# Three projections of the second block in three passes on split operands in place of float32

## The chip, the cores and the metric

The kernel runs on one core of a Trainium2 chip. The metric is the device time of one execution in microseconds, lower is better. Engines are named as in the profile: PE is TensorE (PEld its weight loads), DVE is VectorE, ACT is ScalarE, POOL is GpSimd, SP is SyncE, which here only issues DMAs.

## The reference, cut to what matters

Two transformer blocks follow each other on 512 tokens of width 1024. The change is in the second one's mixer, behind its two attention branches:

```python
def hybrid_mixer(h, positions, w_in, ...):
    ...
    q_lat, kv_lat, k_rope, q_b, k_b, v_b, gate_a, gate_b = jnp.split(h @ w_in, cuts, axis=-1)
    ...
    o_a = mla_attend(q_a, k_a, v_a)                      # 512 wide
    o_b = chunk_band_attend(q_b, k_b, v_b, rel_table)    # 512 wide
    merged = jax.nn.sigmoid(gate_a) * (o_a @ w_oa) + jax.nn.sigmoid(gate_b) * (o_b @ w_ob)
    return merged @ w_out
```

and in the block, `x = x + gt1 * mix`, then an RMS norm, and a mixture of experts.

## The kernel before

All activations are held transposed, features on the 128 partitions and the 512 tokens along the free axis, so a projection takes a 128x128 piece of weights as the stationary operand and a 128x512 piece of activations as the moving one. Each engine has a program of its own, written out by hand in order; they meet by semaphores alone. SyncE streams weights into `ring`, four slots of 2048 columns: a slot holds 256 output columns for 8 (or 4) k steps of 128 rows. `slot()` waits for a slot's load (`full`), `half` (L572) runs one 128-column half of it, `kts` matmuls into one PSUM bank, and counts `half_done`. The load of slot m + 4 waits until both halves of slot m are done. ACT and DVE empty the banks and count `freed["A"]` and `freed["D"]`, for which a later half on the same bank waits; `drain_psum` makes PE wait, ahead of a stage, for all evictions of the stages before.

The order around the change: two attentions of 16 units each (`attend(16, ...)`, the latent one, whose output is `OA`, and `attend(32, ...)`, the banded one, whose output is `OB`). Between units PE also computes the latent gates (`lat_gate_matmuls`, L934), and ACT copies them to `LAT_GATE`. Then:

- `mla_out`, 4 slots: `OA` times `w_oa_2`, 4 k steps, 8 halves. DVE multiplies each with its sigmoid gate (L2131). PE waits for `outed`, 48, before it.
- `band_out`, 8 slots in 4 groups (`gated_projection`): two halves of the band gate, `hT` times `w_in_2` in 8 k steps, then two halves of `OB` times `w_ob_2` in 4 k steps. ACT takes the sigmoid of the gates (L1365), DVE multiplies and adds into `merged2` (L1900, L1901).
- `w_out2`, 4 slots: `merged2` times `w_out_2`, 8 k steps. DVE adds each half to the residual (`residual`, L2000). The norm of the next part follows.

All of it is float32, and each float32 matmul leaves two records in the trace. The first block's attention projections (L880, L904) and its feed-forward part (L1031, L1060) already work in another way: a weight w and an operand x are each held as a rounded part in the type fp32r ("high") and what is left of them ("low"), and three matmuls, low w x high x, high w x low x, high w x high x, take the place of one in float32. There ACT makes the high part of a weight slot (L1383) and DVE the low part in the ring's own slot (L1922); in the feed-forward part GpSimd makes it.

```python
            drain_psum(pe, "w_out2")
            for t in range(4):
                m = slot()
                for hf in range(2):
                    hh = 2 * t + hf
                    if hh >= 4:
                        pe.wait_ge(freed["D"], BEFORE["w_out2"]["D"] + hh - 3)
                    half(m, hf, hh % 4, lambda k: merged2[:, k, :])
```

Of the kernel before, what the change touches and what calls it, by code (L numbers as in the profile page):

```python
# [12 lines left out]
F32 = mybir.dt.float32  # L13
# [3 lines left out]
ALU = mybir.AluOpType  # L17
# [132 lines left out]
def build(nc, a, stop=99):  # L150

    with ExitStack() as ctx:
# [6 lines left out]
        def sem(name):  # L159
            return ctx.enter_context(nc.semaphore(name))  # L160
# [86 lines left out]
        BROW = area(33280, 640)  # L247
        merged2, gate2 = area(6656, KT, T), area(12800, 2, T)
        LAT_GATE = [area(4096 + i * T, T) for i in range(4)] + [area(10752 + i * T, T) for i in range(4)]
        H2T = area(4096, 4, D)  # L250
        XE = area(8192, 2, 8, 2 * SLOTS)
        PICKED = area(10240, 2, 4, 2 * SLOTS)
# [46 lines left out]
        y_made, mean_made, var_made, g_made = sem("y_made"), sem("mean_made"), sem("var_made"), sem("g_made")  # L299
        y_added, centred, y_sq, y_root, y_final = [sem(n) for n in (  # L300
            "y_added", "centred", "y_squared", "y_rooted", "y_final")]
        gate_ready, lat_gate = sem("gate_ready"), sem("latent_gate_ready")
        scored, masked, peaked, probbed, turned, turnedS, weighed, outed, diag_made = [sem(n) for n in (
            "scored", "masked", "peaked", "probbed", "turned", "turned_copied", "weighed", "outed", "diagonal_made")]
# [253 lines left out]
        def _(pe):  # L558
            n = [0]

            def slot():
                m = n[0]
                n[0] += 1
                pe.wait_ge(full[m % R], full_value(m))
                return m
# [267 lines left out]
            pe.wait_ge(y_final, 8)  # L833


            def gated_projection(phase, rhs, kts):
                drain_psum(pe, phase)
                for g in range(4):
                    m = slot()
                    for hf in range(2):  # L840
                        i = 2 * g + hf
                        if i >= 2:
                            pe.wait_ge(freed["A"], BEFORE[phase]["A"] + i - 1)
                        half(m, hf, i % 2, h_)
                    m = slot()
                    for hf in range(2):
                        i = 2 * g + hf
                        if i >= 2:
                            pe.wait_ge(freed["D"], BEFORE[phase]["D"] + i - 1)
                        half(m, hf, 2 + i % 2, rhs, kts=kts)  # L850

            for g in range(4):
                m = slot()
# [265 lines left out]
            attend(32, parts_band, PROB2, PROBT2, gates_beside=2)  # L1119
            pe.wait_ge(outed, 48)  # L1120
            for g in range(4):
                m = slot()
                for hf in range(2):
                    i = 2 * g + hf
                    if i >= 4:
                        pe.wait_ge(freed["D"], BEFORE["mla_out"]["D"] + i - 3)
                    half(m, hf, i % 4, lambda k: OA[:, k, :], kts=4)
            gated_projection("band_out", lambda k: OB[:, k, :], 4)
            drain_psum(pe, "w_out2")
            for t in range(4):  # L1130
                m = slot()
                for hf in range(2):
                    hh = 2 * t + hf
                    if hh >= 4:
                        pe.wait_ge(freed["D"], BEFORE["w_out2"]["D"] + hh - 3)
                    half(m, hf, hh % 4, lambda k: merged2[:, k, :])
            norm_sum(4)
            pe.wait_ge(normed, 5)
            if stop < 6:
# [87 lines left out]
        def _(act):  # L1227
# [124 lines left out]
                if t < 8:  # L1352
                    y_square(t)

            def gates(phase):

                for g in range(4):
                    for hf in range(2):
                        i = 2 * g + hf
                        act.wait_ge(half_done, 2 * FIRST[phase] + 4 * g + hf + 1)  # L1360
                        if i >= 2:
                            act.wait_ge(freed["D"], BEFORE[phase]["D"] + i - 1)
                        elif i == 0:
                            act.wait_ge(freed["D"], BEFORE[phase]["D"])
                        act.activation(gate2[:, i % 2, :], ps[:, i % 2, :], ACT.Sigmoid, bias=ZERO).then_inc(freed["A"], 1)  # L1365

            act.wait_ge(y_final, 8)
            act.activation(C2S, col("c_2", 0, 8), ACT.Silu).then_inc(silu_c, 1)
            act.wait_ge(freed["A"], BEFORE["rw_out"]["A"] + 8)
# [49 lines left out]
            def attend(u0, parts_of, prob, probT, gates_beside=False):  # L1419
                def exp(i, e):  # L1420
                    u = u0 + i
                    pt = parts_of(pairs[i], i)
                    act.wait_ge(peaked, u + 1)
                    p_ = prob[i % 2][e][:, 0:pt["tiles"] * P]
                    act.activation(p_, p_, ACT.Exp, scale=pt["scale"], bias=NM[:, i % 2, e:e + 1],  # L1425
                                   accum_out=DEN[:, i % 2, e:e + 1]).then_inc(probbed, 1)

                def copies(i, e):
                    u = u0 + i
                    n_ = parts_of(pairs[i], i)["tiles"]  # L1430
                    if u >= 2:
                        act.wait_ge(weighed, u - 1)
                    for t_ in range(0, n_, 4):
                        g = turn_n[0]
                        turn_n[0] += 1
                        k = min(4, n_ - t_)
                        act.wait_ge(turned, g + 1)
                        act.activation(probT[i % 2][e][:, t_ * P:(t_ + k) * P], ps[:, 5 + g % 2, 0:k * P],
                                       ACT.Copy).then_inc(turnedS, 1)

                exp(0, 0)
                exp(0, 1)
                for i in range(len(pairs)):
                    for e in range(2):
                        if i + 1 < len(pairs):
                            exp(i + 1, e)
                        copies(i, e)
                    if gates_beside and i % 4 == 3:
                        lat_gate_copy()

            attend(0, parts1, PROB1, PROBT1)
            if stop < 4:
# [110 lines left out]
            attend(32, parts_band, PROB2, PROBT2, gates_beside=True)  # L1563
            act.wait_ge(freed["A"], BEFORE["mla_out"]["A"] + 8)
            for i in range(8):
                act.activation(LAT_GATE[i], LAT_GATE[i], ACT.Sigmoid, bias=ZERO).then_inc(lat_gate, 1)
            gates("band_out")
# [120 lines left out]
        def _(dve):  # L1688
# [202 lines left out]
                    y_centre(t - 1)  # L1891
                ada_rest(2 * t + 1)

            def gated(phase, gate, merged):

                for i in range(8):
                    g, hf = divmod(i, 2)
                    dve.wait_ge(half_done, 2 * FIRST[phase] + 4 * g + 2 + hf + 1)
                    dve.wait_ge(freed["A"], BEFORE[phase]["A"] + i + 1)
                    lk.done(tt(gate[:, i % 2, :], ps[:, 2 + i % 2, :], gate[:, i % 2, :], ALU.mult))  # L1900
                    tt(merged[:, i, :], merged[:, i, :], gate[:, i % 2, :], ALU.add).then_inc(freed["D"], 1)  # L1901
# [41 lines left out]
            def attend(u0, parts_of, prob, OT):  # L1943
                def peaks(i):
                    u = u0 + i
                    pt = parts_of(pairs[i], i)
# [26 lines left out]
                for i in range(len(pairs)):  # L1973
                    if i + 1 < len(pairs):
                        peaks(i + 1)
                    if i >= 1:
                        outs(i - 1)
                    denominators(i)
                outs(len(pairs) - 1)

            dve.wait_ge(got_masks, 16)
# [145 lines left out]
            attend(32, parts_band, PROB2, [OB[:, k, :] for k in range(4)])  # L2127
            for i in range(8):
                dve.wait_ge(half_done, 2 * FIRST["mla_out"] + 8 + i + 1)
                dve.wait_ge(lat_gate, i + 1)  # L2130
                tt(merged2[:, i, :], ps[:, i % 4, :], LAT_GATE[i], ALU.mult).then_inc(freed["D"], 1)  # L2131
            gated("band_out", gate2, merged2)
# [194 lines left out]
```

## Time and profile before

| what | value |
|---|---|
| median of 3 runs | 2627.1 us (2624.62 to 2631.7) |
| the profiled execution | 2626.47 us, its span 2624.7 us |
| mean granted TensorE clock | 0.951 of full speed |
| PE busy | 2365.8 us (90%) |
| PE weight loads busy | 1626.4 us (62%) |
| DVE busy | 1036.6 us (39%) |
| ACT busy | 618.3 us (24%) |
| POOL busy | 219.5 us (8%) |
| the three stages of the change | 2030.63 to 2198.58 us |

A busy PE says that matmuls are in flight, not that they run at the engine's best pace, so the rows below give counts and lengths for the stages. The span runs from the first to the last instruction; the device time is a little longer.

### The profile page before, as it was taken

How to read it: one execution, taken by the hardware profiler on the slowest of the kernel's cores; microseconds unless marked ns; L12 is line 12 of the kernel's file. 1: busy time of each engine (PE TensorE's matmuls, PEld its weight loads, DVE VectorE, ACT ScalarE, POOL GpSimd, SP SyncE). 2: the span in 40 equal slices, each digit the busy share in tenths (PEclk: the TensorE clock that was granted, in tenths of full speed). 3: DMA queues.
4: the chain of work that ended last, by engine and by line, in shares of the span. 5: the costliest groups of instructions: out<-in, count | busy, mean ns of one | idle time of the engine just before them, and what ended most of it. 6: DMA issues, size and time to landing. Idle time of an engine off the chain costs nothing.

```text
span 2624.7 us, 41843 instructions
## 1 busy us (share of the span) xinstructions
PE 2365.8 (90%) x18202; PEld 1626.4 (62%) x18202; DVE 1036.6 (39%) x1878; ACT 618.3 (24%) x922; POOL 219.5 (8%) x97
## 2 busy tenths in 40 slices
PE   8889999999789999889599989789899997899992
PEld 7376859584338898554388868436355443777771
DVE  0264554535565562441477740130544111311113
ACT  1213232312502222540333321210345001111111
POOL 0010101010000000000244334100000000000001
PEclk9899999999899999899799999899999998899996
DMA  6211010104464652003133322441200220699992
GB/s 203 79 35 34 19 49 4 49 13 137 144 206 153 192 183 91 1 31 114 32 97 96 96 72 89 84 100 44 92 17 17 88 76 0 212 361 374 369 339 104
DMA packets 273606, 295.19 MB, mean 112 GB/s; under 512 B 7593, under 2 KB 257361, under 8 KB 273457
## 3 DMA queue, kind: packets, MB, share of 16 engines
q1 hardware_dynamic: 268080, 274.85, 32.4%
q0 software_dynamic: 3072, 9.74, 1.8%
q10 hardware_dynamic: 2304, 8.39, 0.8%
q8 instruction: 122, 2.00, 0.3%
q14 instruction: 28, 0.22, 0.0%
HBM read 279.84 MB, written 13.11 MB: 112 GB/s over the span
## 4 chain that ended last, share of the span: by engine, by line
PE 80%; DVE 11%; ACT 4%; issue 2%; DMA 2%; POOL 0%; SPq 0%; POOLq 0%; DVEq 0%; ACTq 0%
PE ps L572 20%; PE ps L1031 9%; PE ps L661 9%; PE ps L880 7%; PE ps L1060 5%; PE ps L1175 4%; PE ps L1193 4%; PE ps L904 3%; PE ps L589 2%; PE ps L934 2%; PE ps L1212 2%; PE ps L598 2%; PE ps L950 2%; PE ps L962 1%; DVE arena L1951 1%
## 5 line engine op out<-in xcount | busy, mean ns | idle before, releaser
L572 PE MATMUL ps<-hT,ring 128*128 128x512 f32 (+1 forms) x816 | 359.1, 599 | 17.5 <-DVE hT L1740 16.0
L572 PEld LDWEIGHTS ps<-hT,ring 128*128 128x128 f32 (+1 forms) x816 | 154.8, 191 | 218.6 <-issue 200.7
L572 PE MATMUL ps<-arena,ring 128*128 128x512 f32 (+1 forms) x592 | 262.4, 602 | 14.7 <-DVE arena L2105 6.4
L661 PE MATMUL ps<-arena 64*64 64x64 f32 x7168 | 226.1, 221 | 16.2 <-POOL arena L1630 8.8
L661 PEld LDWEIGHTS ps<-arena 64*64 64x64 f32 x7168 | 221.0, 137 | 21.0 <-POOL arena L1630 9.6
L572 PEld LDWEIGHTS ps<-arena,ring 128*128 128x128 f32 (+1 forms) x592 | 111.8, 190 | 160.4 <-issue 146.0
L1636 POOL TENSOR_TENSOR w_low<-ring,w_high 128x2048 fp32r<-128x2048 f32 x22 | 103.8, 4721 | 869.9 <-ACT w_high L1466 869.9
L1031 PE MATMUL ps<-h_high,w_low 128*128 128x512 f32 x352 | 140.2, 398 | 24.2 <-DVE h_low L2010 24.2
L1031 PE MATMUL ps<-h_high,w_high 128*128 128x512 f32 x352 | 140.7, 400 | 0.0
L1031 PE MATMUL ps<-h_low,w_high 128*128 128x512 f32 x352 | 139.3, 396 | 0.0
L1175 PE MATMUL ps<-arena 128*128 128x128 f32 x1088 | 130.5, 279 | 2.9 <-DVE arena L2207 2.9
L1175 PEld LDWEIGHTS ps<-arena 128*128 128x128 f32 x1088 | 125.9, 194 | 9.1 <-issue 6.1
L1193 PE MATMUL ps<-ring,arena 128*64 128x256 f32 x1024 | 118.7, 380 | 2.3 <-DMA ring<-in_w_up 1.5
L1951 DVE CUSTOM_DVE_ANT_0 arena<-ps,arena 128x256 f32<-128x256 f32 (+3 forms) x160 | 67.1, 468 | 128.2 <-PE ps L950 128.0
L880 PE MATMUL ps<-h_high,w_low 128*128 128x512 f32 x256 | 103.1, 403 | 13.1 <-DVE w_low L1922 12.7
L1268 ACT ACTIVATE arena<-ps 128x512 f32<-128x512 f32 x104 | 62.1, 597 | 210.9 <-PE ps L661 200.7
L1193 PEld LDWEIGHTS ps<-ring,arena 128*64 128x64 f32 x1024 | 87.5, 137 | 37.0 <-issue 9.6
L1776 DVE TENSOR_TENSOR arena<-ps,arena 128x512 f32<-128x512 f32 x88 | 60.9, 692 | 119.2 <-PE ps L661 119.1
L2032 DVE TENSOR_TENSOR rstd<-arena 128x512 f32<-128x512 f32 x22 | 98.4, 4473 | 17.5 <-ACT arena L1497 17.5
L880 PE MATMUL ps<-h_low,w_high 128*128 128x512 f32 x256 | 102.3, 400 | 0.0
L880 PE MATMUL ps<-h_high,w_high 128*128 128x512 f32 x256 | 101.9, 398 | 0.0
L1425 ACT ACTIVATE arena<-arena,small 128x384 f32<-128x384 f32 (+6 forms) x96 | 68.0, 708 | 114.9 <-DVE small L1959 114.9
(328 smaller groups left out, 3535.9 us busy)
## 6 DMA issues: line engine op xcount, KB each, us to landing
ring<-in_w_in SPq DMA_DIRECT2D x54, 1024.0 KB, 5.2
arena<-in_w_ada SPq DMA_DIRECT2D x80, 512.0 KB, 4.0
ring<-in_w_gate SPq DMA_DIRECT2D x32, 1024.0 KB, 10.4
ring<-in_w_up SPq DMA_DIRECT2D x32, 1024.0 KB, 11.8
arena<-in_w_down SPq DMA_DIRECT2D x32, 1024.0 KB, 9.2
ring<-in_w_up SPq DMA_DIRECT2D x44, 512.0 KB, 4.5
ring<-in_w_ada SPq DMA_DIRECT2D x8, 1024.0 KB, 8.7
ring<-in_w_down SPq DMA_DIRECT2D x8, 1024.0 KB, 5.0
```

The costliest lines, as they stand in the source:

```text
L572: mm = pe.matmul(dst, w[:, k, hf * P:hf * P + width], rhs(k), start=(start and k == 0), stop=(stop and k == kts - 1))
L661: mm = pe.matmul(ps[r, bank, cc], l[r, cc], x[r, 0:64] if x is eye64 else x[r, cc], start=(i == 0), stop=(i == len(terms) - 1))
L880: mm = pe.matmul(ps[:, bank, :], w_[:, k, hf * P:hf * P + P], x_[:, k, :], start=(k == 0 and i_ == 0), stop=(k == KT - 1 and i_ == 2))
L904: mm = pe.matmul(ps[:, hh % 4, tt * 256:tt * 256 + 256], x_[:, k, tok:tok + P], w_[:, k, :], start=(k == 0 and i_ == 0), stop=(k == KT - 1 ...
L1031: mm = pe.matmul(ps[:, (2 * (m - first) + g) % 4, :], w_[:, k, :], x_[:, k, :], start=(k == 0 and i_ == 0), stop=(k == KT - 1 and i_ == 2))
L1060: mm = pe.matmul(ps[:, hh % 4, :], w_[:, k, hf * P:hf * P + P], x_, start=(kt == 0 and i_ == 0), stop=(kt == FT - 1 and i_ == 2))
L1175: mm = pe.matmul(ps[:, hf, k * P:k * P + P], H2T[:, tt, (4 * hf + k) * P:(4 * hf + k + 1) * P], PICKED[:, par, tt, :], start=(tt == 0), st ...
L1193: mm = pe.matmul(ps[e * SLOTS:(e + 1) * SLOTS, 2 + part, 0:256], XE[:, j, k, e * SLOTS:(e + 1) * SLOTS], w[:, k, :], start=(k == 0), stop= ...
L1425: act.activation(p_, p_, ACT.Exp, scale=pt["scale"], bias=NM[:, i % 2, e:e + 1], accum_out=DEN[:, i % 2, e:e + 1]).then_inc(probbed, 1)
L1636: pool.tensor_tensor(W_LOW[:, slot_, :], ring[:, slot_, :], W_HIGH[:, j % 2, :].bitcast(F32), ALU.subtract).then_inc(w_low, 1)
L1951: dve.tensor_tensor_reduce(out=prob[i % 2][e][:, at:at + mask.shape[1]], in0=out, in1=mask, scale=1.0, scalar=NEG, op0=ALU.add, op1=ALU.ma ...
L2032: tt(val, sil[:, jj % 2, :], cvt[jj % 2][1], ALU.mult).then_inc(dve_link, 1)
```

## The change

The three stages' float32 matmuls become three fp32r matmuls each. Every weight slot and every 128x512 piece of `OA`, `hT` (called H3), `OB` and `merged2` (M2) is split first: ACT copies it to fp32r, DVE subtracts that from it and writes the low part in place. `out_weight(i)` names the 16 slots (0 to 3 `mla_out`, 4 to 11 `band_out` with even ones the gates' and odd ones `OB`'s, 12 to 15 `w_out2`); slots 0 to 3 and `OB`'s have 1024 columns, the others 2048. The high parts take turns in two small buffers (0 to 3) and two large ones (4 to 15), so the cast of weight i waits until PE is done with weight i - 2. `OA`'s pieces and the weights 0 and 1 are split within the band attention; the rest is written into the programs of ACT and DVE among their evictions. PE waits for `out_w_low` at each slot and for `piece_low` at each k step.

```diff
+        OUT_W_HIGH = ([rounded(f"w_small_{i}", offset_of["arena"] + (13824 + i * 1024) * 4, SLOT // 2)[:, :] for i in range(2)]
+                      + [rounded(f"w_large_{i}", offset_of["arena"] + (16896 + i * SLOT) * 4, SLOT)[:, :] for i in range(2)])
...
+        def out_weight(i):
+
+            m = FIRST["mla_out"] + 4 + i
+            size = SLOT // 2 if i < 4 or (i < 12 and i % 2 == 1) else SLOT
+            high = OUT_W_HIGH[i % 2 + (2 if i >= 4 else 0)]
+            return m, high[:, 0:size], ring[:, m % R, 0:size], W_LOW[:, m % R, 0:size]
...
+            def out_slot(i):
+
+                slot()
+                pe.wait_ge(out_w_low, i + 1)
...
+            def out_half(w, hf, bank, pieces, first_piece):
+
+                wl, wh = w
+                n_ = len(pieces)
+                for k, (_, high, low) in enumerate(pieces):
+                    pe.wait_ge(piece_low, first_piece + k + 1)
+                    for i_, (w_, x_) in enumerate(((wl, high), (wh, low), (wh, high))):
+                        mm = pe.matmul(ps[:, bank, :], w_[:, k, hf * P:hf * P + P], x_,
+                                       start=(k == 0 and i_ == 0), stop=(k == n_ - 1 and i_ == 2))
+                mm.then_inc(half_done, 1)
...
             drain_psum(pe, "w_out2")
             for t in range(4):
-                m = slot()
+                w = out_slot(12 + t)
                 for hf in range(2):
                     hh = 2 * t + hf
                     if hh >= 4:
                         pe.wait_ge(freed["D"], BEFORE["w_out2"]["D"] + hh - 3)
-                    half(m, hf, hh % 4, lambda k: merged2[:, k, :])
+                    out_half(w, hf, hh % 4, M2_PIECES, PIECE_AT["M2"])
```

ACT's new program (in the band attention it also makes `OA`'s pieces after units 2, 4, 6, 8 and weights 0 and 1 after units 12 and 14):

```diff
+            def out_weight_high(i):
...
+                act.wait_ge(full[m % R], full_value(m))
+                if i >= 2:
+                    act.wait_ge(half_done, 2 * (m - 2) + 2)
+                act.activation(high, full_, ACT.Copy).then_inc(out_w_high, 1)
...
+            act.wait_ge(outed, 48)
+            for g in range(4):
+                for i in range(2 * g, 2 * g + 2):
+                    act.activation(LAT_GATE[i], LAT_GATE[i], ACT.Sigmoid, bias=ZERO).then_inc(lat_gate, 1)
+                for k in range(2 * g, 2 * g + 2):
+                    high_piece(H3_PIECES[k])
+                if g == 1:
+                    for k in range(4):
+                        high_piece(OB_PIECES[k])
+                out_weight_high(g + 2)
+            for g in range(4):
+                for hf in range(2):
+                    i = 2 * g + hf
+                    act.wait_ge(half_done, 2 * FIRST["band_out"] + 4 * g + hf + 1)
...
+                    act.activation(gate2[:, i % 2, :], ps[:, i % 2, :], ACT.Sigmoid, bias=ZERO).then_inc(freed["A"], 1)
+                out_weight_high(6 + 2 * g)
+                for k in range(2 * g - 2, 2 * g) if g else ():
+                    high_piece(M2_PIECES[k])
+                out_weight_high(7 + 2 * g)
+            for k in range(6, 8):
+                act.wait_ge(freed["D"], BEFORE["band_out"]["D"] + k + 1)
+                high_piece(M2_PIECES[k])
+            out_weight_high(14)
+            out_weight_high(15)
```

DVE's new program (in the band attention, low parts after units 3, 5, 7, 9 and 13, 15):

```diff
+            def out_weight_low(i):
...
+                dve.wait_ge(out_w_high, i + 1)
+                tt(low, full_, high.bitcast(F32), ALU.subtract).then_inc(out_w_low, 1)
...
+            for g in range(4):
+                for k in range(2 * g, 2 * g + 2):
+                    low_piece(H3_PIECES[k])
+                for i in range(2 * g, 2 * g + 2):
+                    dve.wait_ge(half_done, 2 * FIRST["mla_out"] + 8 + i + 1)
+                    dve.wait_ge(lat_gate, i + 1)
+                    tt(merged2[:, i, :], ps[:, i % 4, :], LAT_GATE[i], ALU.mult).then_inc(freed["D"], 1)
+                if g == 1:
+                    for k in range(4):
+                        low_piece(OB_PIECES[k])
+                out_weight_low(g + 2)
+            for g in range(4):
+                out_weight_low(6 + 2 * g)
+                for k in range(2 * g - 2, 2 * g) if g else ():
+                    low_piece(M2_PIECES[k])
+                for i in range(2 * g, 2 * g + 2):
+                    dve.wait_ge(half_done, 2 * FIRST["band_out"] + 4 * g + 2 + i % 2 + 1)
+                    dve.wait_ge(freed["A"], BEFORE["band_out"]["A"] + i + 1)
+                    lk.done(tt(gate2[:, i % 2, :], ps[:, 2 + i % 2, :], gate2[:, i % 2, :], ALU.mult))
+                    tt(merged2[:, i, :], merged2[:, i, :], gate2[:, i % 2, :], ALU.add).then_inc(freed["D"], 1)
+                out_weight_low(7 + 2 * g)
+            low_piece(M2_PIECES[6])
+            low_piece(M2_PIECES[7])
+            out_weight_low(14)
+            out_weight_low(15)
             residual("w_out2", mod2[:, 16:24])
```

## Rows read from the trace of the kernel before

**Rows 1.** The page: busy time, share of the span and instructions of each engine.

```profile
PE 2365.8 (90%) x18202; PEld 1626.4 (62%) x18202; DVE 1036.6 (39%) x1878; ACT 618.3 (24%) x922; POOL 219.5 (8%) x97
```

**Rows 2.** Stretches: length, busy PE, PEld, DVE, ACT, POOL, clock, DMA share, GB/s.

```profile
2030.60:2059.00 28.40, 27.73 (x64) 12.08 (x64) 5.43 (x8) 5.67 (x9) 0.00 (x0) 1.00 0.36 110
2059.00:2142.00 83.00, 82.64 (x192) 36.40 (x192) 9.90 (x16) 5.50 (x8) 0.00 (x0) 1.00 0.26 83
2142.00:2199.00 57.00, 55.17 (x128) 24.24 (x128) 6.91 (x10) 0.00 (x0) 2.86 (x4) 1.00 0.09 24
```

**Rows 3.** Chain of waits in the three stages: start, length (us), what.

```profile
2030.63 27.73 PE ps L572 x64
2059.20 82.64 PE ps L572 x192
2143.39 55.19 PE ps L572 x128
```

**Rows 4.** Chain of waits in earlier projections: split ones, and `w_uk_2`.

```profile
1023.43 22.52 PE ps L880 x96
...
1289.02 249.01 PE ps L1031 x1056
...
1880.06 7.01 PE ps L1113 x16
```

**Rows 5.** Groups by line and shape, of three stretches: busy us, mean ns.

```profile
L880 PEld LDWEIGHTS ps<-h_low,w_high 128*128 128x128 f32 x256 | 48.7, 190 | 11.2
...
L1909 DVE TENSOR_TENSOR h_low<-hT,h_high 128x512 fp32r<-128x512 f32 x8 | 5.1, 682 | 0.0
...
L1373 ACT ACTIVATE h_high<-hT 128x512 fp32r<-128x512 f32 x8 | 4.2, 612 | 0.0
...
L2032 DVE TENSOR_TENSOR rstd<-arena 128x512 f32<-128x512 f32 x22 | 98.4, 4473 | 17.5 <-ACT arena L1497 17.5
...
L2000 DVE SCALAR_TENSOR_TENSOR arena<-ps,small,arena 128x512 f32<-128x512 f32 x8 | 6.0, 750 | 50.1 <-PE ps L572 50.1
...
L1900 DVE TENSOR_TENSOR arena<-ps,arena 128x512 f32<-128x512 f32 x8 | 5.5, 690 | 72.9 <-PE ps L572 72.9
L1365 ACT ACTIVATE arena<-ps,small 128x512 f32<-128x512 f32 x8 | 5.5, 687 | 93.9 <-PE ps L572 93.9
```

**Rows 6.** Order of time at two hand-overs: start, length, what [idle before].

```profile
857.02 0.40 PE L880 MATMUL ps<-h_high,w_high 128*128 128x512 f32 x1
...
857.52 1.92 ACT L1383 ACTIVATE w_high<-ring 128x2048 fp32r<-128x2048 f32 x1 [5.06 <-PE ps L880]
...
859.47 2.29 DVE L1922 TENSOR_TENSOR w_low<-ring,w_high 128x2048 fp32r<-128x2048 f32 x1 [1.32 <-ACT w_high L1383]
...
2142.60 0.69 DVE L1901 TENSOR_TENSOR arena<-arena 128x512 f32<-128x512 f32 x1
```

**Rows 7.** Order of time in the attention's last units.

```profile
2021.77 0.40 ACT L1425 ACTIVATE arena<-arena,small 128x128 f32<-128x128 f32 x1 [2.11 <-DVE small L1959]
...
2024.12 0.29 DVE L1951 CUSTOM_DVE_ANT_0 arena<-ps,arena 128x128 f32<-128x128 f32 x1 [1.34 <-PE ps L950]
...
2029.96 0.29 DVE L1969 COPY arena<-ps 128x128 f32<-128x128 f32 x1 [1.53 <-PE ps L980]
```

**Rows 8.** DMA issues, 2025 to 2200 us: count, KB each, us to landing.

```profile
ring<-in_w_in SPq DMA_DIRECT2D x4, 1024.0 KB, 5.2
```

**Rows 9.** After pauses: TensorE's next matmul, chain of waits, stretches (PEclk).

```profile
613.07 1.13 PE L799 MATMUL ps<-arena,const 128*128 128x512 f32 x2 [3.24 <-DVE arena L1869]
...
1256.03 8.85 PE ps L589 x16
...
2203.05 10.08 PE ps L589 x16
...
610.00:616.00 6.00, 2.93 (x6) 0.97 (x6) 4.68 (x10) 0.00 (x0) 0.00 (x0) 1.00 0.56 175
...
2203.00:2209.00 6.00, 5.95 (x7) 2.52 (x8) 0.00 (x0) 1.28 (x1) 0.00 (x0) 0.50 0.00 0
```

More of the change, by code:

```diff
@@ L301, in build @@
             "y_added", "centred", "y_squared", "y_rooted", "y_final")]
+        out_w_high, out_w_low, piece_high, piece_low = [sem(n) for n in (
+            "out_weights_high", "out_weights_low", "piece_high_made", "piece_low_made")]
         gate_ready, lat_gate = sem("gate_ready"), sem("latent_gate_ready")
@@ L833, in _ @@
             pe.wait_ge(y_final, 8)
-            def gated_projection(phase, rhs, kts):
-                drain_psum(pe, phase)
-                for g in range(4):
-                    m = slot()
[L840 to L850, printed above, removed]
+            def out_slot(i):
+                slot()
+                pe.wait_ge(out_w_low, i + 1)
+                _, high, _, low = out_weight(i)
+                return [v.rearrange("p (k c) -> p k c", c=256) for v in (low, high)]
+            def out_half(w, hf, bank, pieces, first_piece):
[7 more added lines that the diff above has]
+                mm.then_inc(half_done, 1)
             for g in range(4):
@@ L1121, in _ @@
             for g in range(4):
-                m = slot()
+                w = out_slot(g)
                 for hf in range(2):
@@ L1126, in _ @@
                         pe.wait_ge(freed["D"], BEFORE["mla_out"]["D"] + i - 3)
-                    half(m, hf, i % 4, lambda k: OA[:, k, :], kts=4)
-            gated_projection("band_out", lambda k: OB[:, k, :], 4)
+                    out_half(w, hf, i % 4, OA_PIECES, PIECE_AT["OA"])
+            drain_psum(pe, "band_out")
+            for g in range(4):
+                w = out_slot(4 + 2 * g)
+                for hf in range(2):
+                    i = 2 * g + hf
+                    if i >= 2:
+                        pe.wait_ge(freed["A"], BEFORE["band_out"]["A"] + i - 1)
+                    out_half(w, hf, i % 2, H3_PIECES, PIECE_AT["H3"])
+                w = out_slot(5 + 2 * g)
+                for hf in range(2):
+                    i = 2 * g + hf
+                    if i >= 2:
+                        pe.wait_ge(freed["D"], BEFORE["band_out"]["D"] + i - 1)
+                    out_half(w, hf, 2 + i % 2, OB_PIECES, PIECE_AT["OB"])
             drain_psum(pe, "w_out2")
             for t in range(4):
-                m = slot()
+                w = out_slot(12 + t)
                 for hf in range(2):
@@ L1353, in _ @@
                     y_square(t)
[L1355 to L1365, printed above, removed]
             act.wait_ge(y_final, 8)
@@ L1449, in attend @@
                         lat_gate_copy()
+                    if split_beside and i in (2, 4, 6, 8):
+                        act.wait_ge(outed, u0)
+                        high_piece(OA_PIECES[i // 2 - 1])
+                    if split_beside and i in (12, 14):
+                        out_weight_high(i // 2 - 6)
             attend(0, parts1, PROB1, PROBT1)
@@ L1892, in _ @@
                 ada_rest(2 * t + 1)
[L1894 to L1901, printed above, removed]
             for i in range(8):
@@ L1941, in _, with low_piece, attend @@
             lk.done(tt(mod2, ps[:, 6, 32:80], col("b_ada_2", 0, 48), ALU.add))
-            def attend(u0, parts_of, prob, OT):
+            def out_weight_low(i):
+                if i >= 16:
+                    return
+                _, high, full_, low = out_weight(i)
+                dve.wait_ge(out_w_high, i + 1)
+                tt(low, full_, high.bitcast(F32), ALU.subtract).then_inc(out_w_low, 1)
+            pieces_n = [0]
+            def low_piece(piece):
+                pieces_n[0] += 1
+                dve.wait_ge(piece_high, pieces_n[0])
+                tt(piece[2], piece[0], piece[1].bitcast(F32), ALU.subtract).then_inc(piece_low, 1)
+            def attend(u0, parts_of, prob, OT, split_beside=False):
                 def peaks(i):
@@ L1978, in attend @@
                     denominators(i)
+                    if split_beside and i in (3, 5, 7, 9):
+                        low_piece(OA_PIECES[i // 2 - 1])
+                    if split_beside and i in (13, 15):
+                        out_weight_low(i // 2 - 6)
                 outs(len(pairs) - 1)
@@ L2126, in _ @@
             attend(16, parts_mla, PROB2, [OA[:, k, :] for k in range(4)])
[L2127 to L2132, printed above, removed]
+            attend(32, parts_band, PROB2, [OB[:, k, :] for k in range(4)], split_beside=True)
+            for g in range(4):
[9 more added lines that the diff above has]
+                out_weight_low(g + 2)
+            for g in range(4):
+                out_weight_low(6 + 2 * g)
[11 more added lines that the diff above has]
+            out_weight_low(15)
             residual("w_out2", mod2[:, 16:24])
```

29 lines of the change are left out of this document (24 added, 5 removed).

## The prediction

> **What bounds the kernel now.** I read the page first: TensorE works for 2365.8 us, 90% of the span [rows 1]. The table of stretches then shows that in the three stages that the change touches (2030.6 to 2199 us) TensorE is busy without a break at a granted clock of 1.00, while VectorE works 22 and ScalarE 11 of 168 us, and the DMA engines are a third used or less [rows 2]. The chain of waits has the stages as three pieces of TensorE work: 27.73 us for the 32 matmuls of `mla_out` (a float32 matmul leaves two records, so x64), 82.64 us for the 96 of `band_out`, 55.19 us for the 64 of `w_out2`, with pauses of 0.83 and 1.55 us between [rows 3]. So the stretch from 2030.63 to 2198.58, 167.95 us, is as long as its matmuls, 165.56 us for 192 of them, 0.862 us each. What counts is (a) how long the new matmuls take and (b) whether the splitting, all of it new work for ScalarE and VectorE, keeps ahead of them.
>
> **The matmuls.** Each of the 192 becomes three of the kind that the first block already runs: 96 of them in 22.52 us, which is 0.2346 us each, and 1056 in 249.01, 0.2358 [rows 4]. 576 x 0.2346 = 135.1 us, against 165.6: 30.4 us less. I take 0.2346 because its row has no cold start in it. The order and the tile shapes are those of the first block's helper.
>
> The new passes are not as cheap as the old ones: a fourth of 0.862 is 0.2155, and at that price 576 would take 124.1, another 11.0 less. That is a rival below. The Trainium skill ("FP8 and Floating Point Precision", TensorE Precision Notes) says that true float32 is four passes through the array, and the reduced form reads float32 and truncates; counted by passes alone, three for four would save a quarter, 41.4 us. Rows of this kernel say 30.4, and the rows decide.
>
> Each half now also has a wait ahead of every group of three matmuls, 192 in all, on semaphores that have mostly fired. The row of 96 in [rows 4] runs over two weight slots and four halves, with their waits on slot, splitting and bank, at full pace; and eight matmuls of `w_uk_2` with a wait ahead of nearly each take 7.01 us, 0.876 each against 0.862 [rows 4, 3], so at most 0.014 us a wait, 2.7 us for 192. I take 0.
>
> **The splitting, beside the matmuls.** Prices: ScalarE casts 128x512 in 0.61 and 128x2048 in 1.92 us; VectorE subtracts 128x512 in 0.68 and 128x2048 in 2.29 [rows 5, 6]; in proportion between those, 128x1024 takes 1.05 and 1.22. A gate's sigmoid is 0.69, each of VectorE's two operations on a half 0.69 [rows 5]. Handing over costs little: a half's last matmul (857.02, 0.40 long) ends 0.10 before ScalarE's cast starts, VectorE starts 1.95 after the cast started; from VectorE's last addition (2142.60 + 0.69) to the next matmul is 0.10 [rows 6, 3].
>
> Added in all: 24 operand pieces and 16 weights (eight of 1024, eight of 2048 columns): ScalarE 24 x 0.61 + 8 x 1.05 + 8 x 1.92 = 38 us, VectorE 24 x 0.68 + 8 x 1.22 + 8 x 2.29 = 44. Beside 11 and 22 us of old work this is far below 135 us, so the sum fits; what decides is order. I walk it, with 0 at 2030.63 (the last output of the attention). A slot of four k steps is 24 matmuls, 5.63 us; of eight, 11.26.
>
> Within the attention lie OA's four pieces and weights 0 and 1. Their longest pieces, 1.05 on ScalarE and 1.22 on VectorE, stand after units in which ScalarE sits idle 2.11 us and VectorE 1.34 and 1.53 [rows 7]. Cost taken: 0; were all of it exposed, 4 x 1.29 + 2 x 2.27 = 9.7. TensorE starts at 0, as before.
>
> `mla_out`: slots end at 5.63, 11.26, 16.89, 22.52. Weight 2 may be cast once slot 0 is used: 5.73, ready 8.0, wanted at 11.26. Weight 3: ScalarE waits for slot 1, 11.36, VectorE first makes two H3 pieces, two evictions and OB's four, and is ready at 16.0, wanted at 16.89. Weight 4 (2048 columns): slot 2 ends 16.89, cast from 17.0, low part 18.95 to 21.25. VectorE then has H3's pieces 6 and 7 (to 22.6) and the last two evictions (to 24.0), for which the next stage waits: TensorE starts `band_out` at 24.1, a pause of 1.6 against 0.83 before.
>
> `band_out`: weight 6 of the next group can be cast only when slot 4 is used, and is wanted one OB slot, 5.63 us, later. In between: 0.10 to ScalarE, a sigmoid 0.69 queued ahead of the cast, 1.95 to VectorE's start, 2.29, 0.10 = 5.13. It fits with 0.5 us to spare, in each of three groups. The other weights have 11 us. The ring's loads start a ring's turn ahead: 5.2 us for 1024 KB [rows 8], against at least 16.9 between a slot's end and its next use; nothing is exposed. Four groups of 16.89 end at 91.7.
>
> Then the queue order bites. Slot 10 ends at 86.0; ScalarE: sigmoid to 86.8, cast of weight 12, VectorE's low part 88.75 to 91.05, M2's pieces 4 and 5 to 92.4, multiplication and addition for two halves, 4 x 0.69, to 95.2; only then may `w_out2` start, at 95.3. The pause is 3.6 us, against 1.55. Weight 13 (ready 97.5) and M2's last pieces (98.9) come while the first half still works on its first six pieces (until 99.6).
>
> In `w_out2` VectorE's program has the low parts of weights 14 and 15 *ahead of* the residual evictions. Weight 15 takes the buffer of weight 13, so its cast waits for slot 13, the second, to end: 95.3 + 22.52 = 117.8. Cast from 117.9, low part 119.85 to 122.1, the first residual (0.75 [rows 5]) to 122.9. TensorE wants the first bank again at 117.8, for its fifth half, and gets it at 123.0: a pause of 5.2 us that the kernel before does not have. The last two slots end at 145.5.
>
> Sum: 167.95 - 145.5 = 22.4 us less; that is 30.4 less in matmuls, and pauses of 10.4 (1.6 + 3.6 + 5.2) for 2.4.
>
> **The clock.** TensorE's next work after the stretch pauses 4.5 us (2198.58 to 2203.05) for the squares of the norm; its sixteen float32 records, 6.90 at the pace of [rows 3], then take 10.08, and the stretch 2203 to 2209 shows clock 0.50 of 2.4 GHz, so 1.2 [rows 3, 9]; before the pause TensorE was busy at 1.00 [rows 2]. The same records in the first block, behind the same squares, took 8.85. After a pause of 3.24 us the clock was still 1.00 [rows 9]. So the pause of 5.2 us costs a further 1.95 to 3.2; I take 2.4. The one of 3.6 lies between the rows: 0 to 3.2, I take 1.1.
>
> The Trainium skill ("TensorE: Matmul & The Clock Gate", What's actually happening) says that the gate runs freely, not in step with the kernel. By that rule either pause may cost more in one run than in another; the trace agrees in that two such pauses cost 1.95 and 3.2.
>
> **The forecast.** 22.4 - 2.4 - 1.1 = 18.9 us less. The profiled execution took 2626.47 (span 2624.7), the median of the runs is 2627.1. 2626.5 - 18.9 = 2607.6; set toward the median, 2608.0.
>
> **Rivals.**
> *The passes at the old pace.* 0.2155 instead of 0.2346: 2597. Against it stand both split rows of [rows 4]. 6 in 100.
> *Starved of weights.* A subtraction-like operation of 512 columns takes VectorE 4.47 us where GpSimd works beside it [rows 5]. If a weight's low part took as long here, the chain in `band_out` would be 7.3 for a cover of 5.63: three times 1.7, and 2.2 more in each of the three pauses that have one in them, 11.7 in all: 2620. GpSimd is idle here [rows 2], so the full price is unlikely; a part of it, or some us lost in the attention, gives 2611 to 2618. 14 in 100.
> *The pauses hide.* If an eviction comes earlier than walked, or the clock holds, up to 6 us come back: 2602 to 2604. 8 in 100.
> *Slower: the waits between triples.* If a wait keeps the next weights from loading under the matmul before, the load (0.19 [rows 5]) and a hop (0.10) are bare, 192 x 0.29 = 56 us: 2664. It turns into a loss from 18.9 / 192 = 0.10 us a wait. That row allows 0.014 [rows 4]. 4 in 100.
> *No change:* only if one of these just eats 18.9. 2 in 100.
> The walk as it stands, 2604 to 2612: 66 in 100.
>
> A difference under 0.3% (7.9 us) can't be told from none here. Faster by more: 94 in 100. The range runs from 2601, which leaves out the cheap passes, to 2616, which leaves out the upper end of the starved case and the slower one.
>
> **What would show it.** In the profile after: the 576 matmuls at 0.2333 to 0.236 apart; a pause ahead of each of the two later stages near 1.6 and 3.6 us; one of about 5.2 us four halves into `w_out2`, ended by VectorE's residual, with the low part of weight 15 just before it; clock 0.50 behind it for some us; no pause inside `band_out`; the attention as long as before. The prediction is wrong if `band_out` shows a pause at each group, if the triples stand apart by more than 0.71 us, or if TensorE starts `mla_out` later than now.

## The result, and the profile after

The changed kernel took 2602.32 us in the median of 4 runs (2596.43 to 2604.45), against 2627.53 for the kernel before (4 runs, 2624.62 to 2631.7): a ratio of 0.9899 (0.9877 to 0.9921), or 26.5 us less (20.8 to 32.3); the two medians are 25.2 us apart. The forecast was 2608.0 with a range from 2601 to 2616, set from a sum of 18.9 us less; against the 2627.1 it started from, the range is 26.1 to 11.1 us less. As a time 2602.32 lies in the range; as a saving by the ratio, 26.5 lies just outside it. A second comparison, with five more runs of the changed kernel and 17 of the one before, gave 0.9929 (0.9916 to 0.9942), 18.7 us less, close to the forecast. Both have to be explained. One of the 17 took 2854.59 us, at a mean granted clock of 0.822 where the others had 0.95, and no ratio counts it.

The profiled execution of the changed kernel took 2600.65 us, its span 2598.9. Its chain of waits (start, length, what) through the three stages, which answers to [rows 3]:

```profile
1874.53 7.01 PE ps L1139 x16
...
2025.10 22.65 PE ps L874 x96
...
2049.01 67.42 PE ps L874 x288
2116.42 3.22 issue
2119.64 22.63 PE ps L874 x96
2142.36 1.92 ACT w_large L1454
2144.30 2.29 DVE w_low L2010
2147.51 24.81 PE ps L874 x96
2173.14 3.62 ACT hT L1271
```

The stages run from 2025.10 to 2172.32, 147.22 us, where they took 167.95: 20.7 us less. There are three pauses. The one ahead of `band_out` is 1.26 us (2025.10 + 22.65 to 2049.01), that ahead of `w_out2` 3.22, and the one in the middle of `w_out2` lies between 2142.27 and 2147.51, 5.24 us, with the cast of weight 15 and then its low part in it. The two pieces of 96 matmuls in `w_out2` are the same work, yet one took 22.63 and the other 24.81. And `mla_out` starts 5.5 us earlier than before. The attention is not the reason: from the first matmul of `w_uk_2`'s group (L1139) to the start of `mla_out` it is 150.57 us, in [rows 3, 4] as well (1880.06 to 2030.63).

VectorE's queue around the two later pauses, with ScalarE's cast of weight 12, in order of time (start, length, instruction, idle before it):

```profile
2111.46 1.91 ACT L1454 ACTIVATE w_large<-ring 128x2048 fp32r<-128x2048 f32 x1
...
2113.39 2.29 DVE L2010 TENSOR_TENSOR w_low<-ring,w_large 128x2048 fp32r<-128x2048 f32 x1 [9.51 <-ACT w_large L1454]
2115.60 1.28 DVE L2018 TENSOR_TENSOR merged_low<-arena,merged_high 128x512 fp32r<-128x512 f32 x2
...
2116.81 0.68 DVE L2227 TENSOR_TENSOR arena<-ps,arena 128x512 f32<-128x512 f32 x1
...
2118.85 0.69 DVE L2228 TENSOR_TENSOR arena<-arena 128x512 f32<-128x512 f32 x1
...
2144.30 2.29 DVE L2010 TENSOR_TENSOR w_low<-ring,w_large 128x2048 fp32r<-128x2048 f32 x1 [8.89 <-ACT w_large L1454]
2146.51 2.72 DVE L2081 SCALAR_TENSOR_TENSOR arena<-ps,small,arena 128x512 f32<-128x512 f32 x4
```

This is the chain that was walked: weight 12's low part, two pieces of M2, the four operations of the last two halves, and TensorE starts 0.10 after the last; later, weight 15's low part with all the residuals behind it. The stretches show the clock, in the columns of [rows 2]:

```profile
2119.60:2147.50 27.90, 22.62 (x96) 17.97 (x97) 8.84 (x7) 4.43 (x3) 2.85 (x4) 0.96 0.12 26
2147.50:2153.00 5.50, 5.49 (x14) 4.39 (x15) 1.73 (x3) 0.00 (x0) 0.00 (x0) 0.57 0.00 0
2153.00:2173.00 20.00, 19.31 (x83) 15.20 (x81) 2.90 (x4) 0.00 (x0) 0.00 (x0) 1.00 0.00 0
```

Behind the pause of 5.2 us TensorE works 5.5 us at a mean of 0.57, at 1.2 GHz for most of it, and then at 1.00 again. Behind the one of 3.22 there is nothing of the kind: the 96 matmuls there take 22.63 us, like the 96 of `mla_out`.

### The profile page after: what moved, and what is told of

Same layout as the page of the kernel before. It is cut to its first block, busy times and chain, and to the rows that moved or that the text cites. A ratio compares the mean times of both kernels' runs of the same rounds, so it can differ in the third digit from the quotient of the medians.

```text
span 2598.9 us, 42348 instructions
## 1 busy us (share of the span) xinstructions
PE 2333.0 (90%) x18394; PEld 1660.6 (64%) x18394; DVE 1076.9 (41%) x1918; ACT 653.6 (25%) x962; POOL 219.3 (8%) x97
## 4 chain that ended last, share of the span: by engine, by line
PE 79%; DVE 11%; ACT 4%; issue 2%; DMA 2%; POOL 0%; SPq 0%; POOLq 0%; DVEq 0%; ACTq 0%
PE ps L596 14%; PE ps L1057 10%; PE ps L685 9%; PE ps L906 7%; PE ps L874 5%; PE ps L1086 5%; PE ps L1214 4%; PE ps L1232 4%; PE ps L930 3%; PE ps L613 2%; PE ps L960 2%; PE ps L1251 2%; PE ps L622 2%; PE ps L976 2%; DVE arena L2028 1%
## 5 line engine op out<-in xcount | busy, mean ns | idle before, releaser
L596 PE MATMUL ps<-hT,ring 128*128 128x512 f32 (+1 forms) x688 | 304.5, 602 | 16.7 <-DVE hT L1810 16.0
L596 PEld LDWEIGHTS ps<-hT,ring 128*128 128x128 f32 (+1 forms) x688 | 131.0, 191 | 187.3 <-issue 169.4
L596 PE MATMUL ps<-arena,ring 128*128 128x512 f32 (+1 forms) x336 | 149.8, 603 | 12.4 <-DVE arena L2186 6.4
L596 PEld LDWEIGHTS ps<-arena,ring 128*128 128x128 f32 (+1 forms) x336 | 62.9, 189 | 95.7 <-issue 82.4
L906 PE MATMUL ps<-h_high,w_low 128*128 128x512 f32 x256 | 102.6, 401 | 13.6 <-DVE w_low L1983 13.1
## 6 DMA issues: line engine op xcount, KB each, us to landing
ring<-in_w_gate SPq DMA_DIRECT2D x32, 1024.0 KB, 10.4
```

The source lines that it names most:

```text
L596: mm = pe.matmul(dst, w[:, k, hf * P:hf * P + width], rhs(k), start=(start and k == 0), stop=(stop and k == kts - 1))
L906: mm = pe.matmul(ps[:, bank, :], w_[:, k, hf * P:hf * P + P], x_[:, k, :], start=(k == 0 and i_ == 0), stop=(k == KT - 1 and i_ == 2))
```

## The experiments

Eight runs, two of the known kernels again and six of new ones, in two groups: a0, a1, e1 and e2 beside a kernel before with a median of 2626.87 us, e3, e4, e5 and e7 beside one of 2625.27. The stage length is that of the chain, from the first matmul of `mla_out` to the end of the last piece of `w_out2`.

| kernel | `mla_out` starts | stages | median us | ratio to before |
|---|---|---|---|---|
| before | 2030.63 | 167.95 | 2627.53 | 1 |
| after | 2025.10 | 147.22 | 2602.32 | 0.9899 (0.9877 to 0.9921) |
| a0_before_again | 2027.49 | 167.95 | 2623.28 | 0.9991 (0.9981 to 1.0002) |
| a1_after_again | 2032.17 | 147.22 | 2607.53 | 0.9929 (0.9916 to 0.9942) |
| e1_low15_after_residual3 | 2030.60 | 139.61 | 2597.79 | 0.9891 (0.9875 to 0.9906) |
| e2_w_out2_float32 | 2031.91 | 148.07 | 2605.58 | 0.9921 (0.9908 to 0.9933) |
| e3_filled_pause | 2032.11 | 144.88 | 2603.16 | 0.9909 (0.9891 to 0.9927) |
| e4_evictions_first | 2032.42 | 139.72 | 2594.62 | 0.9883 (0.9866 to 0.9901) |
| e5_one_wait_per_half | 2031.94 | 147.23 | 2605.67 | 0.9922 (0.9904 to 0.9940) |
| e7_low_parts_by_gpsimd | 2029.95 | 153.00 | 2606.44 | 0.9916 (0.9897 to 0.9936) |

**Both kernels again.** No edit.

> The kernel before, once more. The profile of after reached the first matmul of `mla_out` 5.5 us earlier than that of before (2025.10 against 2030.63), though nothing in the program ahead of it differs but the splitting inside the band attention. Theory A (chance): stretches that start on a slow TensorE clock run shorter or longer from one execution to the next, so this profile may reach `mla_out` anywhere from 2024 to 2033 us, and the ratio to before is 1.000. Theory B (the change itself moves the first part): this profile has `mla_out` at 2030.6 again, within 1 us, and every profile with the change at 2025.

> The changed kernel, once more, in five rounds. Theory A: the stretch from the first matmul of `mla_out` to the last of `w_out2` is 147.2 us again within 1 us (167.95 before), so 20.7 us is what the change is worth, and the ratio comes nearer to 1 - 20.7/2627 = 0.992 than to the first 0.9899; `mla_out` starts anywhere from 2019 to 2030 us. Theory B: the ratio stays at 0.990 and `mla_out` starts at 2025 again.

The stages are 167.95 and 147.22 us again, to the hundredth, while their start moved: to 2027.49 in the kernel before, to 2032.17 in the changed one, where before it was the changed one that was early. The eight profiles with the change or a version of it start `mla_out` between 2025.10 and 2032.42, the two without at 2027.49 and 2030.63. So the 5.5 us are chance, and theory B falls. The range expected for the changed kernel, 2019 to 2030, was too low: 2032.17 lies outside it.

Most of what separates the two profiles of the changed kernel at `mla_out`, 7.1 us, comes from one pause far ahead of the change. Near 610 us TensorE waits for VectorE, and then runs a few matmuls, up to those of L815. The first profile, and then the second, with its stretch there in the columns of [rows 2]:

```profile
610.74 1.13 PE L823 MATMUL ps<-arena,const 128*128 128x512 f32 x2 [3.28 <-DVE arena L1939]
615.69 0.98 PE ps L815 x28
```

```profile
613.81 2.07 PE L823 MATMUL ps<-arena,const 128*128 128x512 f32 x2 [3.28 <-DVE arena L1939]
623.30 1.01 PE ps L815 x28
613.80:623.30 9.50, 9.49 (x12) 2.91 (x14) 3.75 (x8) 0.00 (x0) 0.00 (x0) 0.50 0.59 176
```

After the same pause of 3.28 us the clock stayed at 1.00 in one profile and fell to 0.50 in the other, and the same work took 4.95 us in one and 9.49 in the other. This is the pause of 3.24 us that the prediction read in the kernel before [rows 9]. In the ten profiles of this document it is 3.17 to 3.47 us long; the clock held behind it in three (before, a0, after) and fell in the seven others, at a price of 1.7 to 4.5 us.

Between the kernel before and the first profile of the changed one that pause makes no difference. A part of their 5.5 us can be seen in the first attention (stretches of the kernel before, and then of the changed one, from the last projection slots ahead of it to the first matmul behind it):

```profile
1023.40:1167.10 143.70, 120.21 (x1002) 88.39 (x1001) 62.13 (x291) 68.15 (x135) 0.00 (x0) 0.95 0.04 12
```

```profile
1018.70:1159.80 141.10, 117.41 (x1002) 87.09 (x1001) 62.12 (x291) 67.95 (x135) 0.00 (x0) 0.98 0.04 12
```

The same 1002 records of matmuls, VectorE and ScalarE busy for the same time within 0.2 us; the clock was 0.95 in one and 0.98 in the other, and 2.6 us went with it. In the second profile of the changed kernel this stretch is 143.5 us at 0.95. The lead of the first profile goes up and down on the way: 3.1 us at the first projection (72.23 against 75.34), 0.7 at 223.35, 4.7 at 1018.71, 7.3 at 1159.80, 5.5 at `mla_out`. The first projection begins at 72.2 to 72.3 in seven of the eight changed kernels, and at 75.3 to 75.7 in e1 and both profiles of the kernel before. Whether that has to do with the program is open. Near 224 us, at the third of these projection pieces, 0.3 to 2.4 us are left of it: the eight start it at 221.96 to 223.73, the two of the kernel before at 224.06 and 224.34.

**The low part of weight 15 behind the residuals.**

```diff
-            out_weight_low(15)
-            residual("w_out2", mod2[:, 16:24])
+            residual("w_out2", mod2[:, 16:24], between=lambda: out_weight_low(15))
```

with `between` called ahead of the fifth residual.

> VectorE makes the low part of weight 15 after the fourth residual, not ahead of the first. The walk's account: the pause of 5.25 us halfway through `w_out2` goes, and with it the slow clock behind it (x96 in 24.81 against 22.63), so the stages take 147.2 - 5.25 - 2.2 = 139.8 us, and the kernel 7.4 us less than with the change alone. Rival (the pause is due to the bank or to slot 14's weights, not to the order of VectorE's queue): a pause of 3 to 5 us stays, and less than 2 us is won.

The chain of waits of this kernel in `w_out2`:

```profile
2121.94 3.22 issue
2125.16 45.05 PE ps L874 x192
```

192 matmuls in one piece: the pause is gone and the clock's price with it. The stages take 139.61 us, expected 139.8. The rival falls. The medians of e1 and a1, which ran in one group, are 9.7 us apart, where the stages give 7.6; another 2.3 lie behind the stages, which the expectation did not count: from the end of `w_out2` to the end of the span it is 424.0 us in e1 and 426.3 in a1, and the 16 matmuls behind the norm's pause (L613) take 8.84 us against 10.20.

**`w_out2` in float32.**

```diff
-                w = out_slot(12 + t)
+                m = slot()
...
-                    out_half(w, hf, hh % 4, M2_PIECES, PIECE_AT["M2"])
+                    half(m, hf, hh % 4, lambda k: merged2[:, k, :])
```

with the pieces of M2 and the weights 12 to 15 no longer split.

> Only `w_out2` goes back to float32; `mla_out` and `band_out` stay split. By the walk `w_out2`'s part of the change has eaten itself up: 10.1 us won in 192 fp32r matmuls for 64 float32 ones, 5.25 lost in the pause, 2.2 to the clock, 1.7 more pause ahead of the stage. So the stages take 91.3 + 1.6 + 55.2 = 148.1 us, within 1 us of the changed kernel's 147.2, and the times can't be told apart. Rival (each stage brings its share of the 20.7 us, a third of the matmuls a third of the gain): 7 to 10 us slower than the changed kernel.

The stages take 148.07 us, 0.85 more than with `w_out2` split: a third of the new matmuls brings 4% of the gain. The rival falls. The saving in matmuls is 55.19 - 45.29 = 9.9 us (22.63 and, without the slow clock, 22.66 from e3); 5.24 goes back in the pause within the stage, 1.66 in the longer pause ahead of it, and 2.15 to the clock. The ratios, 0.9921 and 0.9929, can't be told apart.

**The pause filled.** Ahead of the wait of `w_out2`'s fifth half:

```diff
+                    if hh == 4:
+                        for _ in range(20):
+                            pe.matmul(ps[:, 5, :], M2_HIGH[:, 0, 0:P], M2_HIGH[:, 0, :], start=True, stop=True)
```

> As the changed kernel, but TensorE runs 20 matmuls of 512 columns into an unused bank while it would pause halfway through `w_out2`. The pause before the fifth half stays as long, since VectorE sets it, but TensorE isn't idle in it. If the 2.2 us that the half stretch behind the pause takes over the others (24.8 against 22.6) are the slow clock, they go: that piece takes 22.6, the stages 145.0 against 147.2, and the granted clock stays at 1.00. Rival (they are slot 14's or 15's weights coming late): 24.8 stays.

TensorE's and the other engines' instructions in order of time there:

```profile
2149.12 4.71 PE L1175 MATMUL ps<-merged_high 128*128 128x512 f32 x20
2149.38 1.92 ACT L1457 ACTIVATE w_large<-ring 128x2048 fp32r<-128x2048 f32 x1 [9.28 <-PE ps L874]
2151.32 2.29 DVE L2013 TENSOR_TENSOR w_low<-ring,w_large 128x2048 fp32r<-128x2048 f32 x1 [8.90 <-ACT w_large L1457]
2153.54 2.72 DVE L2084 SCALAR_TENSOR_TENSOR arena<-ps,small,arena 128x512 f32<-128x512 f32 x4
2154.33 0.50 PE L874 MATMUL ps<-merged_high,w_low 128*128 128x512 f32 x1 [0.51 <-DVE arena L2084]
```

and its chain behind the pause:

```profile
2154.33 22.66 PE ps L874 x96
```

The wait is as long as it was (2149.12 to 2154.33, 5.2 us), but with TensorE at work in it the next 96 matmuls take 22.66 us and not 24.8, and the granted clock is 1.00 in both stretches, as expected. So the 2.2 us were the clock's, and nothing late is behind them. 144.88 us, expected 145.0.

**Evictions first.** The edit of e1, and VectorE's order in the last groups: in `mla_out` the pieces 6 and 7 of H3 behind the last two evictions, in `band_out` weight 12 between the evictions of the seventh and the eighth half, and the rest behind both, with TensorE's waits counted to match:

```diff
+                if g == 3:
+                    for k in range(6, 8):
+                        low_piece(H3_PIECES[k])
...
+                    if i == 7:
+                        out_weight_low(12)
...
+            for k in range(4, 8):
+                low_piece(M2_PIECES[k])
+            out_weight_low(13)
```

> E1, and VectorE also empties banks ahead of what is not yet due: in the last group of `mla_out` both evictions before H3's pieces 6 and 7, in the last group of `band_out` the seventh half's before weight 12's low part and the eighth's right behind it, then M2's pieces 4 to 7, then weight 13. By the walk the pause ahead of `band_out` falls from 1.26 to 0.9, the one ahead of `w_out2` from 3.2 to 2.1: the stages take 138.3 us, 1.5 less than E1. Rival (the low part of weight 12 sets the start alone, so the order of the evictions doesn't matter): the same length as E1 within 0.3 us. The ratio to before should be near 1 - 29.6/2627 = 0.9887 where upstream chance allows.

139.72 us, where 138.3 was expected and e1 had 139.61. By its length alone the rival would have won. The chain says otherwise:

```profile
2032.42 22.65 PE ps L874 x96
...
2055.90 64.64 PE ps L874 x276
...
2124.82 0.70 DVE arena L2237
2125.53 0.09 issue
2125.62 4.51 PE ps L874 x12
```

The pause ahead of `band_out` is 0.83 us (from 2055.07), as expected 0.9. The one ahead of `w_out2` is 2.28, expected 2.1, and 3.22 in e1. But this time the clock fell to 1.2 GHz behind it, as the stretch behind the pause shows:

```profile
2125.60:2128.70 3.10, 3.08 (x7) 2.48 (x8) 3.10 (x5) 0.78 (x2) 2.61 (x4) 0.50 0.87 254
```

The 192 matmuls took 46.52 us, 1.47 more than e1's 45.05. Without that the stages would be 138.25. At this place the pause of 3.22 us, in five profiles (3.21 in e5), never cost clock, and this shorter one did, while the pause of 3.2 to 3.5 us near 610 us cost it in seven of ten. There is one profile of e4, so how often its pause does so is not known, and what the reordering is worth stays open between -0.1 and 1.4 us; the ratio, 0.9883 (0.9866 to 0.9901), is the lowest measured, but it can't be told from e1's.

**Fewer waits.** OA, H3 and OB wait once at each half:

```diff
+                if first_piece < 16:
+                    pe.wait_ge(piece_low, first_piece + n_)
                 for k, (_, high, low) in enumerate(pieces):
-                    pe.wait_ge(piece_low, first_piece + k + 1)
+                    if first_piece >= 16:
+                        pe.wait_ge(piece_low, first_piece + k + 1)
```

> For OA, H3 and OB, TensorE waits for the last piece once at each half instead of for each piece at each k step: 104 of the 192 waits fall away, and all these pieces are ready by then. If a wait that has fired costs nothing between triples, the two pieces of TensorE work keep 22.65 and 67.4 us. If each cost 0.014 us, the bound that I took from the w_uk_2 matmuls, 1.5 us less in all.

The two pieces take 22.67 and 67.44 us, against 22.65 and 67.42. A wait between triples, once it has fired, costs nothing that can be measured here, and the rival of the prediction that ended on the slower side has no ground.

**The low parts of the weights 6 to 15 by GpSimd.** VectorE's routine skips them.

```diff
+            for i in range(6, 16):
+                _, high, full_, low = out_weight(i)
+                pool.wait_ge(out_w_high, i + 1)
+                pool.wait_ge(out_w_low, i)
+                pool.tensor_tensor(low, full_, high.bitcast(F32), ALU.subtract).then_inc(out_w_low, 1)
```

> GpSimd makes the low parts of weights 6 to 15, VectorE those of 0 to 5 and all operand pieces. It takes 4.72 us for 2048 columns in the feed-forward part. So in `band_out` the chain from a gate slot's end to the next gate weight is 0.10 + 0.69 + 1.95 + 4.72 + 0.10 = 7.6 for a cover of 5.63: three pauses of 1.9 us. VectorE's residuals no longer stand behind weight 15, so the pause in `w_out2` and the clock behind it go, 7.4 us. Walk: 147.2 + 5.8 - 7.4 = 145.6 us, with the pause ahead of `w_out2` as before. Rival (VectorE and GpSimd hold each other up, as where a 512-column operation of VectorE takes 4.47 us beside GpSimd): VectorE's evictions stretch to 2 to 4.5 us wherever they meet, GpSimd's to over 5, and the stages take over 150.

The stages take 153.00 us, 7.4 more than walked: the rival is right. The pause within `w_out2` went, as expected. The chain has a pause at each group of `band_out`, of 1.69 us where 1.9 was walked:

```profile
2053.86 17.03 PE ps L874 x72
2070.89 1.69 issue
```

and ahead of `w_out2` one that the walk did not have. In order of time:

```profile
2124.05 4.58 POOL L1740 TENSOR_TENSOR w_low<-ring,w_large 128x2048 fp32r<-128x2048 f32 x1 [11.35 <-ACT w_large L1454]
2124.52 5.26 DVE L2023 TENSOR_TENSOR merged_low<-arena,merged_high 128x512 fp32r<-128x512 f32 x2 [8.61 <-ACT merged_high L1457]
...
2129.12 5.01 POOL L1740 TENSOR_TENSOR w_low<-ring,w_large 128x2048 fp32r<-128x2048 f32 x1 [0.49 <-ACT w_large L1454]
2129.71 0.68 DVE L2232 TENSOR_TENSOR arena<-ps,arena 128x512 f32<-128x512 f32 x1
2130.42 4.27 DVE L2233 TENSOR_TENSOR arena<-arena 128x512 f32<-128x512 f32 x1
```

VectorE's subtraction of two pieces, 1.28 us in the changed kernel, takes 5.26 while GpSimd's operation lasts; its addition of two tiles of SBUF takes 4.27 instead of 0.69. The multiplication between them, which reads one operand from PSUM, takes 0.68 in the midst of GpSimd's next operation. So the last evictions, for which TensorE waits, were held up twice, and it paused 9.1 us ahead of `w_out2` (about 2127.0 to 2136.12) where it had paused 3.22; the clock fell behind it, and the 192 matmuls took 46.83 us against e1's 45.05. The Trainium skill ("SBUF — State Buffer", Who interferes with whom) says that a VectorE instruction with two inputs in SBUF contends with a GpSimd instruction that reads SBUF, over ports that one of the two holds alone, and that one with at most one SBUF input (outside the two-port modes) does not. The trace agrees, with 4.27 and 0.68 us. GpSimd's operation was longer too, 5.01 us where others took 4.58. The times alone would have hidden it, for this kernel's ratio, 0.9916, is no worse than the changed kernel's second one, though its stages are 5.8 us longer. That ratio is worth 22.1 us (16.8 to 27.1) and the stages are 14.95 shorter than before; 1.9 of the rest lies behind the stages, and what is left, 5.3 in the middle of the interval, lies ahead of them or is chance.

## Why the prediction was right or wrong

**The matmuls: right.** 576 at 0.2346 were to take 135.1 us; they took 22.65 + 67.42 + 22.63 + 22.66 = 135.4, the last piece taken from e3, without the slow clock. The passes at the old pace fall.

**The splitting in the attention and in `band_out`: right.** The attention is as long as before. No group of `band_out` pauses: its 288 matmuls are one piece. The half microsecond to spare is real but thin: with GpSimd's 4.6 us in the place of VectorE's 2.29, 2.3 more, each of the three groups paused 1.69, so the spare was 0.6.

**The pauses: right in place and cause, a little too long.** 1.6 was 1.26, 3.6 was 3.22, 5.2 was 5.2; 9.7 in all for 10.4. The walk was too long by small overlaps that it left out: in the rows above, an operation starts up to 0.1 before the end that the row before it has, and in the walk each starts at that end or later.

**The clock: the size of one term off.** Behind the pause of 5.2 us 2.4 was taken and 2.2 measured. Behind the one of 3.6, 1.1 was taken, between bounds of 0 and 3.2; it cost nothing in any of the five profiles with a pause of 3.22. The lower bound rested on one row, the pause of 3.24 us behind which the clock held, and that row was one outcome of two: behind the same pause the clock fell in seven of ten profiles. So a price by the length of the pause alone has no ground, and that it was 0 here is known from these profiles, not understood.

Together the stages were to become 18.9 us shorter and became 20.7 shorter: the 0.7 of the pauses, 1.35 of the clock, less 0.25 of the matmuls. The walk was good to a tenth of what it forecast.

**The range: wrong.** The step that failed is the one that has no term in the sum: "The forecast" took the profiled execution's own time and subtracted from it, so all that lies ahead of the stages counted as fixed. It isn't. The kernels with the change reach `mla_out` anywhere within 7.3 us (2025.10 to 2032.42), with nothing different in their programs ahead of it; one pause near 610 us alone, with the clock falling behind it or not, is worth up to 4.5 of them. For the same reason one of the prediction's signs of being wrong, a later start of `mla_out`, says nothing: five of the eight profiles start it later than 2030.63, with an attention as long as before. And four runs of the changed kernel can have a median 5 us from that of the next five (2602.32 and 2607.53). The range's lower end, 2601, was built from terms of the stages alone and left 7 us below the forecast for both the stages' own error, 1.8, and this chance. The prediction names a noise of 7.9 us, but only for telling the change from none, and doesn't widen the range by it. The first comparison, 26.5, needed 5.8 us of chance beside the 20.7 and used the range up. The second needed 2.0 the other way: that its 18.7 meets the forecast's 18.9 is luck, since the forecast was 1.8 short. Taken from the stage lengths, which repeat to 0.01 us, the change is worth 20.7 us, 0.79%; the second ratio's interval, 15.2 to 22.1 us, holds it, and the first's ends just above it, at 20.8. So the first result is read as 20.7 from the change and 5.8 from chance. That the profiled execution gained 5.5 ahead of the change, and that no later profile of the changed kernel has them again, is shown; for the other three runs of the median it is inferred, and where the 5.5 come from is known only in part.

## What to carry to other kernels

When matmuls are made cheaper by work for other engines, the sum of that work says little; what counts is the chain from the end of one use of a buffer to the next weight wanted, and what is queued ahead of the evictions that TensorE waits for. One low part written ahead of the residuals instead of among them cost 7.6 us in the stages, three quarters of the 9.9 that the split matmuls of that stage save. Compare the length of the changed stretch in two profiles before trusting a difference of medians: here it repeats to 0.01 us, while the first four runs of the changed kernel differ by 8 us and its nine runs by 13.6.

## What the runs showed that was not expected

- A pause of 2.28 us (e4) was followed by 1.2 GHz, and one of 3.22 us at the same place, in five profiles, was not. Behind another, of 3.28 us in both profiles of the changed kernel, the clock held in one and fell in the other. In these rows, between 2.28 and 3.47 us, the length of a pause doesn't say whether the clock falls.
- Most of the difference between two executions of the changed kernel, 4.5 of 7.1 us, comes from that one pause ahead of the change.
- A third of a split product is not a fourth of a float32 one: an fp32r matmul of 512 columns takes 0.2346 us, a fourth of a float32 matmul 0.2155 (165.56 us for 192). The filling matmuls of e3, all with one pair of operands, have the fp32r pace too, 20 in 4.71 us. Why was not tried.
